# TensorE's general path moved ahead of its program, its last scatter in halves, and the sums of the feed-forward squares on GpSimd

## The reference, cut to what matters

```python
    h_lat = h_lat + g2 * hier_moe(modulate(rmsnorm(h_lat, norm_ffn[layer]), sh2, sc2), *moe_args)
    return rmsnorm(h_lat, norm_final)
...
def _sq_relu_mlp(h, w_ff_in, w_ff_out):
    return jnp.square(jax.nn.relu(h @ w_ff_in)) @ w_ff_out
...
        x = x + _sq_relu_mlp(_rms_norm(x, norm3_g[l]), w_ff_in[l], w_ff_out[l])
```

## Time and profile before

| | |
|---|---|
| median of three runs | 1184.34 us |
| profiled execution, its own time | 1182.25 us |
| span of the profiled execution | 1180.5 us |
| TensorE, matmuls (PE) | 1127.4 us, 96% |
| TensorE, weight loads (PEld) | 842.5 us, 71% |
| VectorE (DVE) | 549.6 us, 47% |
| ScalarE (ACT) | 309.3 us, 26% |
| GpSimd (POOL) | 25.4 us, 2% |

### The profile page before, as it was taken

The page is one execution under the profiler, slowest core; times in us unless marked ns, Lnnn a source line. Parts: engine busy times, 40 slices in busy tenths (PEclk is TensorE's granted clock), DMA queues, the critical chain, the costliest instruction groups (busy, mean ns, idle before and its releaser), DMA issues.

```text
span 1180.5 us, 16972 instructions
## 1 busy us (share of the span) xinstructions
PE 1127.4 (96%) x6932; PEld 842.5 (71%) x6932; DVE 549.6 (47%) x1171; ACT 309.3 (26%) x722; POOL 25.4 (2%) x43
## 2 busy tenths in 40 slices
PE   8999999999999999989999999889878989999998
PEld 6689888988777888865555554476756858997443
DVE  2344344414535676441222222236886445677555
ACT  4360010135213301132111110144475241321000
POOL 0000000000000030000000000010000000000000
PEclk9999999999999999989999999999989999999999
DMA  9951112322388535556999999932410423444540
GB/s 381 400 221 72 72 72 76 135 80 103 124 325 335 210 148 206 210 208 267 425 426 426 425 426 426 366 130 72 144 36 2 178 71 108 174 183 179 178 143 36
DMA packets 34732, 241.92 MB, mean 205 GB/s; under 512 B 3947, under 2 KB 4203, under 8 KB 6365
## 3 DMA queue, kind: packets, MB, share of 16 engines
q1 hardware_dynamic: 33500, 234.46, 50.2%
q0 software_dynamic: 720, 3.12, 0.7%
q10 hardware_dynamic: 432, 3.23, 0.7%
HBM read 239.74 MB, written 1.05 MB: 204 GB/s over the span
## 4 chain that ended last, share of the span: by engine, by line
PE 87%; DVE 4%; ACT 4%; DMA 2%; SPq 1%; issue 1%; DVEq 0%; ACTq 0%
PE bank L1406 20%; PE bank L1403 11%; PE bank L1789 10%; PE bank L1383 8%; PE bank L2147 8%; PE bank L1816 5%; PE bank L1454 4%; PE bank L1751 3%; PE bank L1758 2%; DMA arena<-in_stream 2%; PE bank L1374 2%; PE bank L1474 1%; PE bank L1639 1%; PE bank L1642 1%; PE bank L1587 1%; PE bank L2124 1%
## 5 line engine op out<-in xcount | busy, mean ns | idle before, releaser
L1406 PE MATMUL bank<-ring,arena 128*128 128x256 f32 x784 | 174.2, 379 | 1.0 <-ACT arena L1226 0.7
L1406 PEld LDWEIGHTS bank<-ring,arena 128*128 128x128 f32 x784 | 148.1, 190 | 21.3 <-ACT arena L1226 1.0
L818 ACT ACTIVATE arena<-bank 128x256 f32<-128x256 f32 x90 | 32.5, 381 | 194.1 <-PE bank L1406 159.7
L1383 PE MATMUL bank<-ring,arena 128*128 128x256 f32 x320 | 71.0, 380 | 0.2 <-DMA ring<-in_stream 0.2
L1383 PEld LDWEIGHTS bank<-ring,arena 128*128 128x128 f32 x320 | 60.3, 190 | 9.5 <-issue 0.8
L1403 PE MATMUL bank<-arena,ring 128*128 128x128 f32 x528 | 63.0, 275 | 0.0
L1403 PEld LDWEIGHTS bank<-arena,ring 128*128 128x128 f32 x528 | 61.7, 192 | 0.5
L1789 PE MATMUL bank<-ring,arena 128*64 128x256 f32 x512 | 57.0, 381 | 0.0
L1383 PE MATMUL bank<-ring,hTl 128*128 128x256 f32 x256 | 56.6, 379 | 0.0
L1383 PEld LDWEIGHTS bank<-ring,hTl 128*128 128x128 f32 x256 | 48.3, 190 | 8.1 <-issue 1.9
L1789 PEld LDWEIGHTS bank<-ring,arena 128*64 128x64 f32 x512 | 36.0, 137 | 24.1 <-issue 6.7
(11 more groups left out here) (517 smaller groups left out, 1878.5 us busy)
## 6 DMA issues: line engine op xcount, KB each, us to landing
ring<-in_stream SPq DMA_DIRECT2D x163, 1024.0 KB, 7.2
arena<-in_stream SPq DMA_DIRECT2D x38, 1024.0 KB, 13.1
hTl<-in_stream SPq DMA_DIRECT2D x9, 1024.0 KB, 11.0
hTc<-in_stream SPq DMA_DIRECT2D x9, 1024.0 KB, 12.8
consts<-in_consts ACTq DMA_DIRECT2D x1, 3081.0 KB, 16.7
arena<-in_mem SPq DMA_DIRECT2D x2, 512.0 KB, 4.8
arena<-in_x SPq DMA_DIRECT2D x1, 1024.0 KB, 18.4
arena<-in_ctx SPq DMA_DIRECT2D x1, 1024.0 KB, 23.8
```

The source lines that it names most:

```text
L818: ins = act.activation((p[:, 0, :], p[:, 1, :], first)[n], b, ACT.Copy)
L1383: mm = pe.matmul(b[:, 256 * i:256 * i + 256], h[:, k, 128 * i:128 * i + 128], w[:, k, :], start=(k == 0), stop=(k == KD - 1))
L1406: mm = pe.matmul(b, lhs(*source, k), rhs[:, k, :], start=(start and k == 0), stop=(k == 3), skip_group_check=True)
```

## The change

- TensorE's functions `experts`, `scatter_half`, `last_scatter` and `further_rounds` are defined first. Its program begins with a jump over the body of the general path, which now lies ahead of the program. After the last pair of experts a compare-and-branch goes back to that body if `over` is set, and otherwise to the instruction behind it, the last scatter.
- The last scatter waits for each half of the columns by itself and raises `main.added` after each; ScalarE and DVE wait for the half that they copy.
- The waits and the memset that the last scatter had needed in the general path go from ScalarE's and DVE's bodies.
- `squares_summed` for all eight pairs and the weight sums for q = 0 and 1 (`first_sums`) go from DVE to GpSimd, with a semaphore `pool_summed`. GpSimd's order is: squares 0 to 5, weight sums 0 and 1, squares 6 and 7.

```diff
+            def squares_summed(p):
+                f = ffh[:, 4 * p:4 * p + 4, :].rearrange("p (j n) t -> p j n t", j=2)
+                s = fsum[:, 2 * p:2 * p + 2, :]
+                pool.wait_ge(ff_ready, p + 2)
+                pool.tensor_tensor(s[:, :, 0:256], f[:, :, 0, :], f[:, :, 1, :], ALU.add)
+                pool.tensor_tensor(s[:, :, 256:384], f[:, :, 0, 0:128], f[:, :, 1, 128:256], ALU.add)
+                pool.tensor_tensor(s[:, :, 384:512], f[:, :, 0, 128:256], f[:, :, 0, 0:128], ALU.subtract)
+                pool.tensor_tensor(s[:, :, 512:640], f[:, :, 1, 0:128], f[:, :, 1, 128:256], ALU.subtract).then_inc(pool_summed, 2)
+            def first_sums(q):
+                n = len(FREED) - 16 + q
+                w = ring[:, n % RING, :].rearrange("p (k n) -> p k n", k=2)
+                w67, w1, w3, w4 = wsum[q]
+                pool.wait_ge(tile_loaded[n % RING], 16 * (n // RING + 1))
+                pool.tensor_tensor(w3, w[:, 0, 512:1024], w[:, 1, 512:1024], ALU.subtract)
+                pool.tensor_tensor(w4, w[:, 1, 0:512], w[:, 0, 0:512], ALU.subtract)
+                pool.tensor_tensor(w1, w[:, 0, 0:512], w[:, 1, 512:1024], ALU.add)
+                pool.tensor_tensor(w67, w[:, :, 0:512], w[:, :, 512:1024], ALU.add).then_inc(pool_summed, 1)
+            for p in range(6):
+                squares_summed(p)
+            first_sums(0)
+            first_sums(1)
+            squares_summed(6)
+            squares_summed(7)
...
-            act.wait_ge(main.added, 1)
             for n in range(2):
+                act.wait_ge(main.added, n + 1)
                 act.activation(hlat[:, 1, 512 * n:512 * n + 512], acc[2 + n][:, :], ACT.Copy).then_inc(u_act, 1)
...
+            def last_scatter(added):
+                for n in range(2):
+                    pe.wait_ge(main.y_taken, 2 * PAIRS + 1 + n)
+                    for j in range(NT):
+                        mm = scatter_half(j, n, QUADS - 1)
+                    mm.then_inc(added, 1)
...
+            pe.br("pe_first")
+            with nc.body("pe_more", valid_engines=[mybir.EngineType.PE]):
+                further_rounds()
+                pe.br("pe_last")
+            first = nc.switch_bb("pe_first")
...
             over = pe.value_load(over_i[0:1, 0:1], min_val=0, max_val=1)
-            main_last()
-            with pe.If(over > 0):
...
+            pe.br_ne(over, 0, on_true="pe_more", on_false="pe_last")
+            nc.switch_bb("pe_last", parent=first.parent)
             t.n += MOE_RING
+            last_scatter(main.added)
...
             for q in range(14):
                 tile()
-                pe.wait_ge(rows_folded, FOLDED_ROWS[FOLDED[-1]] + q + 1)
+                pe.wait_ge(pool_summed, q + 1 if q < 12 else 16)
                 plain_products(q, (2, 5))
                 if q == 0:
                     pe.wait_ge(sum_taken, len(SUMS))
-                pe.wait_ge(weights_folded, 4 * len(FOLDED) + q + 1)
+                if q < 2:
+                    pe.wait_ge(pool_summed, 13 + q)
+                else:
+                    pe.wait_ge(weights_folded, 4 * len(FOLDED) + q - 1)
                 summed_products(q, (3, 4, 1, 7, 6))
...
             for p in range(1, 8):
                 weights_fold(f"fp{p}", *ring_tiles(FF_AT + 2 * p))
-                squares_summed(p - 1)
                 blocks_summed(f"fp{p}", [parts_f], [ff_block(p)])
-                if p == 7:
-                    weight_sums(0)
-                    weight_sums(1)
-                    squares_summed(7)
             for q in range(2, 16):
                 weight_sums(q)
```

More of the change, by code:

```diff
@@ new lines, in scatter_half @@
+            def scatter_half(j, n, quad):
+                return pe.matmul(acc[2 * j + n][:, :], hT_PT[j][:, 256:384],
+                                 expert_rows(j, quad)[:, 512 * n:512 * n + 512],
+                                 start=False, stop=False, skip_group_check=True)
+            def last_scatter(added):
+                for n in range(2):
+                    pe.wait_ge(main.y_taken, 2 * PAIRS + 1 + n)
+                    for j in range(NT):
+                        mm = scatter_half(j, n, QUADS - 1)
+                    mm.then_inc(added, 1)
@@ new lines, in further_rounds @@
+            def further_rounds():
+                for s_ in (more.g_done, more.u_done, more.y_ready, more.y_ready) * 2:
+                    pe.matmul(bank[3][0:1, 0:2], ident[:, 0:1], ident[:, 0:2], start=True, stop=True).then_inc(s_, 1)
+                pe.wait_ge(main.y_taken, 2 * PAIRS + 2)
+                with pe.Fori(0, L // CAP - 1) as r:
+                    for j in range(NT):
+                        for n in range(2):
+                            mm = scatter_half(j, n, QUADS - 1)
+                    mm.then_inc(more.added, 1)
+                    experts(more, r, more_loaded, more_spare, lambda s: 16)
+                    pe.wait_ge(more.y_taken, r * (2 * PAIRS + 2) + (2 * PAIRS + 2))
@@ L1829, in _ @@
             pe.wait_ge(xn_ready, 2)
-            main_last = experts(main, 0, tile_loaded, spare_loaded, lambda s: 16 * ((MOE_AT + s) // RING + 1))
+            experts(main, 0, tile_loaded, spare_loaded, lambda s: 16 * ((MOE_AT + s) // RING + 1))
             pe.wait_ge(over_ready, 1)
             over = pe.value_load(over_i[0:1, 0:1], min_val=0, max_val=1)
-            main_last()
-            with pe.If(over > 0):
-                for s_ in (more.g_done, more.u_done, more.y_ready, more.y_ready) * 2:
-                    pe.matmul(bank[3][0:1, 0:2], ident[:, 0:1], ident[:, 0:2], start=True, stop=True).then_inc(s_, 1)
-                with pe.Fori(0, L // CAP - 1) as r:
-                    experts(more, r, more_loaded, more_spare, lambda s: 16)()
+            pe.br_ne(over, 0, on_true="pe_more", on_false="pe_last")
@@ L2736, in _ @@
             with dve.If(over > 0):
[L2737 to L2738 removed]
                 with dve.Fori(0, L // CAP - 1) as r:
                     experts(more, r, False)
[L2741 to L2742 removed]
             for n in range(2):
+                dve.wait_ge(main.added, n + 1)
                 dve.tensor_copy(hlat[:, 0, 512 * n:512 * n + 512], acc[n][:, :]).then_inc(u_dve, 1)
```

154 lines of the change are left out of this document (66 added, 88 removed).

## The result

The changed kernel takes 1190.91 us, median of 6 runs (1185.98 to 1194.1); the kernel before took 1183.51 in 6 runs beside it (1181.76 to 1186.05). The ratio on record is 1.0050, 95% interval 1.0033 to 1.0068: slower. The direction is right and the number lies in the stated range, but the sum behind it is not right: its largest term was far too large, and a loss of about 4 us stood where it had written 0. The profiled execution of after has a span of 1191.6 us and a mean granted clock of 0.984 (before: 1180.5 and 0.993), so it lies 11.1 us above its counterpart, more than the runs as a whole. First the page's part 1.

The account below looks back on a forecast made before the run. TensorE, busy 1127.4 of 1180.5 us, was taken as the bound. Terms -1.8 + 7.6 + 0 = +5.8 us gave 1188.1 on the profiled execution, 1190.1 on the median; stated 1189.0, slower, range 1181.5 to 1195.

Parts of the forecast that it names:

- The wait at the first summed product: Between the two feed-forward matrices: TensorE's 1.82 us wait for DVE's weight sums goes once GpSimd makes them earlier, -1.8 us.
- what was named as next in line: At the same step: sum_taken of the last pair, its releaser running while TensorE still does the four plain matmuls.
- The meeting of GpSimd and DVE: In folded pairs fp1 to fp7: GpSimd's sums delay DVE's subtractions in turn, TensorE idles +7.6 us, bounds 0 and 13.
- General path ahead: At the start: TensorE's jump makes it 1.0 us late, nearly all regained by a later data wait; 0, bounds 0 and 1.
- The last scatter by halves: Hand-over after the experts: DVE's copy stays late by its own branch, so TensorE gains 0 us, bounds -4.3 and 0.
- Rival B: In the folded pairs: GpSimd's sums fit in without delaying DVE, -1.8 us; 0.25, shared with contention under half its size.
- Rival C: Hand-over after the experts: DVE's copy follows the scatter's first half, TensorE goes on 4.3 us earlier; chance 0.12.
- D: Hand-over: 4.4 us of idle time can bring 3.4 us at half clock, costing 1.7 us on top of any case.
- E: TensorE's compare after the experts: if the code behind it needs a fetch, +0.7 us on top of any case.

Follow-up runs that it names:

- e1: The kernel before with only the squares' sums and first two weight sums moved from DVE to GpSimd; 1184.33 us, ratio 1.0001.
- e8: e1 with GpSimd's sums held back until DVE's weight folds of the next or last pair are done; 1181.81 us, ratio 0.9973 to the kernel before.
- e4: The kernel before with only TensorE's general path laid ahead of its program, last scatter undivided, sums on DVE; 1187.71 us, ratio 1.0020.
- e2: The changed kernel without its GpSimd part, all sums on DVE as before; 1188.81 us, ratio 1.0040 to the kernel before.
- e3: The kernel before with only the last scatter done by halves; 1185.64 us, ratio 1.0005.
- e5: e2 with TensorE's general path laid behind its program instead of ahead of it; 1185.53 us, ratio 0.9996 to the kernel before.
- e6: e5 with DVE's general path laid behind DVE's program too; 1179.48 us, ratio 0.9951 to the kernel before.
- e7: e6 with the last scatter undivided; 1183.16 us, ratio 0.9970 to the kernel before.
- e9: The changed kernel with TensorE's and DVE's general paths behind their programs and GpSimd's sums held back as in e8; 1179.41 us, ratio 0.9953 to the kernel before.
- e11: The changed kernel, GpSimd's sums not held back, with TensorE's and DVE's general paths behind their programs; 1180.76 us, ratio 0.9960 to the kernel before.
- e12: The kernel before with only DVE's general path laid behind DVE's program; 1185.01 us, ratio 0.9996.

## Why the prediction was right, and where it was not

- **The wait at the first summed product (-1.8 us): right.** It is gone in after, e1 and e8, and what was named as next in line did not come up: e8's feed-forward is 2.05 us shorter.
- **The meeting of GpSimd and DVE (+7.6 us): the mis-sized term. It is 2.03 us** (e1 against before, with the 1.82 us added; 2.26 against e8). The order in turn was right, the price of a turn was not. I added up recorded durations, 1.31, 1.14, 0.75 and 1.22 us for the four turns behind L2331. From end to end they are 1.12, 1.08, 0.58 and 1.08 us, because alone the rows have 1.27, 0.73 and 1.22 us and in turn each row's first 0.14 to 0.15 us lies under the end of the other engine's. That puts L2335 0.56 us earlier: its delay is 5.09 - 3.70 = 1.39 us, just at the 1.36 us of slack, and 0.7 us a pair becomes 0.1. With a slack that small against four such turns, half a microsecond decides. In fp7 the same shorter turns let GpSimd's last addition of the first weight sum end 0.96 us behind L2331's start, where I had 2.6, and the wait there is 1.18 us, not 2.7. The exclusive lock of the Trainium skill (SBUF — State Buffer, "Who interferes with whom") agrees with this trace: in fp2 and in fp7 no subtraction of DVE ends less than 1.07 us after GpSimd's addition. For the DVE operations that read PSUM that page's other case holds as well (in after L2365 takes 0.41 us beside a GpSimd addition, 0.42 alone). Rival B, at 25%, was the nearest in its number, net +0.21 us where it had -1.8, but not in its mechanism: DVE was delayed.
- **General path ahead (0, bounds 0 and 1): the step that failed.** "The start is quieter than 763 us, so I take 0." The DMA share in the gap of after is 99.5% for the weights' queue alone, and the price was 4.3 to 5.4 us at the first group. I had taken one stall, hidden under the first wait for data. There are two: the jump's own, 3.96 us, hidden as said, and one behind it, which the trace shows as one matmul, 4.41 us of idle time, and an instruction packet; I read it as the fetch of the next code. It makes 2.4 to 5.2 us in the runs (e4, e2 and e3, e2 and e5) and is the largest part of the change's loss that an experiment shows.
- **The last scatter by halves (0): right, and for the reason given.** DVE's copy was 5.23 us late by its own taken branch; e6 shows the cause, e7 what the halves are worth without it. Bound -4.3 was Rival C; e6's hand-over gained 4.01 us over e5's. The row of 5.66 us was weighed rightly against the block of 256 instructions in the Trainium skill (Runtime: NRT & Kernel Launch, "Instruction fetch mechanics"): the body skipped has fewer, and the taken branch stalled DVE all the same, by 5.0 to 6.0 us in nine traces; where it falls through (e6, e9, e11) the copy follows after 0.49 us of waiting for the scatter.
- **D (half clock after the longer idle stretch): came in the profile, larger than its price.** 6.8 us at 0.50 instead of 3.4; the 16 transposes and the group behind them took 3.67 and 8.31 us for 1.97 and 7.08, so 2.9 us for the 1.7 stated. It was left out of the sum as a mere addition.
- **E (branch after the experts not free): did not come**, 100 ns.

The sum as it turned out (0.50% of 1185 us is 5.9): about +4 us for the start, +0.2 for the sums, -0.4 at the hand-over (11.08 against 11.51), and some 2 us that no experiment shows by itself. Half clock is what I put them down to: the mean clock of the 6 runs of after is 0.9875, of the 31 runs of before that stand beside e1 to e4 0.9897, and 0.0022 at 0.7 us for each 0.001 is 1.5 us, an estimate. Three of the six runs of after have 0.984, one of the 86 of before has; which part of the change brings that is open. Two errors, 5.6 us too much in one term and 4 too little in another, met at the right total. That was luck, and a reader should not take the hit for a confirmation.

## What to carry to other kernels

Code that is not run costs where it lies, here 2.4 to 5.2 us at the start and 4.0 at the hand-over: put a rarely taken path behind the last instruction of each engine that has one, so that the normal way takes no branch, neither at the start under full DMA queues nor at a hand-over. Look for a late instruction with no releaser just behind a branch; when two engines have it at the same place, take away both: here either one alone (e5, e12) moved nothing. And when work goes to GpSimd beside DVE additions of two SBUF operands, release it by DVE's own progress rather than by its data: here that turned +0.2 us in the feed-forward into -2.05. When two engines take turns, price a turn from end to end in a trace where they meet, not by the durations that each has alone.

## What the hardware showed that was not expected

- A taken branch stalls DVE by 5.0 to 6.0 us (nine traces) and TensorE by 6.04 to 6.50 us (five traces) at the hand-over, where the DMA share is 0.81 to 0.92; at the start, TensorE's jump is recorded with 3.60 to 3.96 us (three traces) and a second stall of 3.9 to 5.2 us follows one matmul later.
- DVE (additions of two SBUF operands, 1024 elements) and GpSimd in each other's way: DVE 1.07 us longer for a GpSimd addition of 512 elements (1.27 us alone), and GpSimd's 256 elements 1.71 us for 0.73. They go in turn, each turn 0.14 to 0.15 us shorter than the row alone.
- The feed-forward of 195.3 us, in which TensorE's longest wait is 1.8 us, came out within 0.02 us in the nine kernels whose sums are on DVE, while two stages of untouched code differed by 3.5 and 8.9 us. A stage length from one profile each told 0.2 us apart where 12 timed runs told 1.5. Part of the scatter goes with the granted clock: 0.7 us a run for each 0.001 of its mean.
